# Two-layer hybrid backbone on one core: keys and values projected first, queries projected per pair of heads inside the attention loop

## The reference, cut to what matters

```python
def mla_q(cq, g, w_uq, rope):
    q = (rmsnorm(cq, g) @ w_uq).reshape(B, L, 8, 64 + 32)      # 384 -> 8 x 96
    q_nope, q_pe = q[..., :64], q[..., 64:]
    if rope is not None: q_pe = apply_rope(q_pe, ...)           # latent tokens only
    return concatenate([q_nope, q_pe], axis=-1)
def mla_kv(ckv, kpe, g, w_ukv, rope):
    kv = (rmsnorm(ckv, g) @ w_ukv).reshape(B, L, 8, 64 + 64)    # 256 -> 8 x 128
    ...                                                         # keys, values, one rotary key for all heads
def attention(q, k, v):
    s = einsum('bqhd,bkhd->bhqk', q, k) * SM_SCALE
    return einsum('bhqk,bkhd->bqhd', softmax(s), v)
```

## Time and profile before

| | us |
|---|---|
| median of 3 runs (lowest, highest) | 1796.88 (1796.58, 1798.57) |
| the profiled execution | 1798.49 |
| its span, first to last instruction | 1796.7 |
| TensorE busy | 1679.5 (93%) |
| VectorE busy | 1207.2 (67%) |
| ScalarE busy | 898.4 (50%) |

### The profile page before, as it was taken

The page is one execution under the profiler, slowest core; times in us unless marked ns, Lnnn a source line. Parts: engine busy times, 40 slices in busy tenths (PEclk is TensorE's granted clock), DMA queues, the critical chain, the costliest instruction groups (busy, mean ns, idle before and its releaser), DMA issues.

```text
span 1796.7 us, 19966 instructions
## 1 busy us (share of the span) xinstructions
PE 1679.5 (93%) x7740; PEld 1286.2 (72%) x7740; DVE 1207.2 (67%) x1598; ACT 898.4 (50%) x1032; POOL 14.2 (1%) x30
## 2 busy tenths in 40 slices
PE   5998979989999999888878999999999999999996
PEld 2774446767777777676548777878787878878775
DVE  3824554545343444483556899888898989888897
ACT  3323263322122221242355777777777777777764
POOL 1000000000000000000000000000000000000000
PEclk8999999999999999989898999999999999999998
DMA  9125211444444345232023899999998999999993
GB/s 392 58 94 212 115 67 47 169 167 153 150 141 141 117 168 185 94 133 92 24 86 141 305 361 336 345 355 351 349 345 340 358 362 348 346 342 352 361 343 115
DMA packets 55861, 402.48 MB, mean 224 GB/s; under 512 B 6416, under 2 KB 6448, under 8 KB 8784
## 3 DMA queue, kind: packets, MB, share of 16 engines
q1 hardware_dynamic: 53712, 387.47, 57.8%
q0 software_dynamic: 2048, 13.65, 2.0%
HBM read 400.05 MB, written 1.05 MB: 223 GB/s over the span
## 4 chain that ended last, share of the span: by engine, by line
PE 68%; DVE 12%; ACT 4%; issue 2%; DMA 1%; DVEq 0%; ACTq 0%
PE PS L439 19%; PE PS L441 19%; PE PS L440 19%; DVE w_lo L2268 5%; ACT w_hi L1506 3%; PE PS L449 1%; PE PS L733 1%; PE PS L1010 1%; PE PS L760 1%; DVE small L1925 1%; DVE w_lo L1629 1%; PE PS L746 1%; ACT w_hi L1131 1%; DVE arena L1938 1%; PE PS L470 1%
## 5 line engine op out<-in xcount | busy, mean ns | idle before, releaser
L2268 DVE TENSOR_TENSOR w_lo<-arena,w_hi 128x2048 fp32r<-128x2048 f32 x132 | 301.6, 2290 | 43.9 <-ACT w_hi L1506 43.9
L2268 DVE TENSOR_TENSOR w_lo<-raw,w_hi 128x2048 fp32r<-128x2048 f32 x129 | 294.9, 2290 | 32.8 <-ACT w_hi L1506 32.3
L1506 ACT CAST w_hi<-arena 128x2048 fp32r<-128x2048 f32 x132 | 251.5, 1908 | 47.0 <-PE PS L441 47.0
L1506 ACT CAST w_hi<-raw 128x2048 fp32r<-128x2048 f32 x129 | 246.8, 1916 | 44.4 <-PE PS L441 44.4
L439 PE MATMUL PS<-hT_hi,w_hi 128*128 128x512 f32 (+1 forms) x576 | 221.4, 384 | 9.3 <-DVE hT_lo L1760 8.4
L441 PE MATMUL PS<-hT_hi,w_lo 128*128 128x512 f32 (+1 forms) x576 | 215.5, 374 | 0.0
L440 PE MATMUL PS<-hT_lo,w_hi 128*128 128x512 f32 (+1 forms) x576 | 215.1, 373 | 0.0
L439 PE MATMUL PS<-w_hi,hT_hi 128*128 128x512 f32 (+1 forms) x448 | 178.3, 398 | 0.3 <-DVE w_lo L2268 0.3
L441 PE MATMUL PS<-w_hi,hT_lo 128*128 128x512 f32 (+1 forms) x448 | 174.6, 390 | 0.0
L440 PE MATMUL PS<-w_lo,hT_hi 128*128 128x512 f32 (+1 forms) x448 | 173.6, 387 | 0.0
L1629 DVE TENSOR_TENSOR w_lo<-raw,w_hi 128x2048 fp32r<-128x2048 f32 (+1 forms) x54 | 122.6, 2270 | 64.5 <-ACT w_hi L1131 64.0
(11 more groups left out here) (318 smaller groups left out, 2572.2 us busy)
## 6 DMA issues: line engine op xcount, KB each, us to landing
raw<-in_moe SPq DMA_DIRECT2D x132, 1024.0 KB, 6.7
arena<-in_moe SPq DMA_DIRECT2D x132, 1024.0 KB, 6.7
raw<-in_ada SPq DMA_DIRECT2D x45, 1024.0 KB, 4.8
raw<-in_ffn SPq DMA_DIRECT2D x33, 1024.0 KB, 4.8
raw<-in_out SPq DMA_DIRECT2D x8, 1024.0 KB, 5.5
raw<-in_inb SPq DMA_DIRECT2D x8, 960.0 KB, 5.8
raw<-in_ina SPq DMA_DIRECT2D x5, 1024.0 KB, 4.8
arena<-in_hyc POOLq DMA_DIRECT2D x2, 1920.0 KB, 11.2
```

Of the source, the lines that this page charges most:

```text
L1506: nc.scalar.copy(w_hi[:, x_slot(j), :], x_raw(n)).then_inc(x_hi, 1)
L2268: v.tensor_tensor(w_lo[:, x_slot(j), :], x_raw(NGR * (i % 2) + j), w_hi[:, x_slot(j), :].bitcast(F32), ALU.subtract).then_inc(x_lo, 1)
```

## The change

Keys are projected first, then the queries of two pairs, then the values. The other pairs are projected inside the attention loop, two pairs ahead of the pair in work, one head of the pair at a time (256 columns each, side by side in one bank). Queries are held by pair in a ring of three. VectorE saves a pair in one operation (context) or four (latent, in two parts) and does so within odd heads. The query weights and latents now have to live through the loop, so prob, probT, qtmp and qT move, probT in four pieces; the turned probabilities use banks 3 and 4, the queries 5 (pair 1: 4). POOL's last loads wait for `pv 1 3`. The rotary table holds its cosine and sine twice side by side.

```diff
-        qT = A(15616, HEADS, 512)
+        qT = A(15616, 3, 512)
-        qtmp = A(6144, 256)
-        prob = A(7936, 4, 512)
-        probT = A(9984, 4, 4, 256)
+        qtmp = A(6144, 512)
+        prob = A(11008, 4, 512)
+        probT = [A(17152, 4, 256), A(18176, 4, 256), A(14592, 4, 256), A(6656, 4, 256)]
@@ TensorE
+            def query(l, streams, pair, j):
+                s, h = attention_plan(streams)[0][2 * pair + j]
+                if j == 0:
+                    state["q"] = bank(f"q {l} {pair}", 4 if pair == 1 else 5)
+                for k in range(KQ):
+                    i = mm(state["q"][:, 256 * j:256 * j + 256], wuq[:, k, h, :], cqT[:, k, 256 * s:256 * s + 256],
+                           start=k == 0, stop=k == KQ - 1)
+                if j:
+                    i.then_inc(pe_done, 1)
+                    did(f"q {l} {pair}")
@@ TensorE, latents
-                for h in range(HEADS):
-                    o = bank(f"q {l} {h}")
-                    for k in range(KQ):
-                        i = mm(o[:, sp], wuq[:, k, h, :], cqT[:, k, sp], start=k == 0, stop=k == KQ - 1)
-                    i.then_inc(pe_done, 1)
-                    did(f"q {l} {h}")
                 for k in range(KKV):
                     eng.wait_ge(act_done, after(f"ckvTs {l} {k}"))
                 for pr in range(4):
...
+                for pair in range(2):
+                    query(l, streams, pair, 0)
+                    query(l, streams, pair, 1)
                 for t in range(NT):
@@ TensorE, attention
-                    eng.wait_ge(dve_done, after(f"qTs {l} {h}"))
+                    eng.wait_ge(dve_done, after(f"qTs {l} {n // 2}"))
...
-                    o = bank(f"pT {l} {u}", 3 + u % 3)
+                    o = bank(f"pT {l} {u}", 3 + u % 2)
...
                         ahead_to(first[n] + half + 3)
+                        if n // 2 + 2 < len(heads) // 2 and (s == 0 or half != n % 2):
+                            query(l, streams, n // 2 + 2, n % 2)
                         turn_p(n, half)
@@ VectorE
+            def save_query(l, streams, pair, part):
+                heads, units, first = attention_plan(streams)
+                q, own = qT[:, pair % 3, :], bank_of(f"q {l} {pair}")
+                if part == 0:
+                    eng.wait_ge(pe_done, after(f"q {l} {pair}"))
+                    if pair >= 3:
+                        eng.wait_ge(pe_done, after(f"s {l} {first[2 * pair - 4] - 1}"))
+                if heads[2 * pair][0] == 0:
+                    if part == 0:
+                        v.tensor_scalar(q[0:96, :], own[0:96, :], SM_SCALE, None, ALU.mult).then_inc(dve_done, 1)
+                        did(f"read q {l} {pair}", f"qTs {l} {pair}")
+                elif part == 0:
+                    v.tensor_scalar(q[0:64, :], own[0:64, :], SM_SCALE, None, ALU.mult).then_inc(dve_done, 1)
+                    did()
+                    v.tensor_tensor(q[64:96, :], own[64:96, :], ropeq[64:96, :], ALU.mult).then_inc(dve_done, 1)
+                    did()
+                else:
+                    v.tensor_tensor(qtmp[64:96, :], own[96:128, :], ropeq[96:128, :], ALU.mult).then_inc(dve_done, 1)
+                    eng.wait_ge(dve_done, did(f"read q {l} {pair}"))
+                    v.tensor_tensor(q[64:96, :], q[64:96, :], qtmp[64:96, :], ALU.add).then_inc(dve_done, 1)
+                    eng.wait_ge(dve_done, did(f"qTs {l} {pair}"))
@@ VectorE, latents: the five operations per head (L1895 to L1909) go, and in their place
+                for pair in range(2):
+                    save_query(l, streams, pair, 0)
+                    save_query(l, streams, pair, 1)
@@ VectorE, attention
                     share(u - 1)
                     n, j = units[u - 1]
+                    if n % 2 and n // 2 + 2 < len(heads) // 2:
+                        save_query(l, streams, n // 2 + 2, j)
+                        if heads[n][0] == 0:
+                            save_query(l, streams, n // 2 + 2, 1)
@@ POOL
-            eng.wait_ge(pe_done, after("s 1 15"))
-            eng.wait_ge(pe_done, after("pT 1 15"))
+            eng.wait_ge(pe_done, after("pv 1 3"))
@@ tables
-    rq[64:96, 0:256] = COS.T * SM_SCALE
-    rq[96:128, 256:512] = SIN.T * SM_SCALE
+    rq[64:96] = np.tile(COS.T * SM_SCALE, (1, 2))
+    rq[96:128] = np.tile(SIN.T * SM_SCALE, (1, 2))
```

More of the change, by code:

```diff
@@ L732, in score @@
                         q = slice(0, 512) if s else slice(256 * t, 256 * t + 256)
-                        i = mm(o[:, q], qT[0:96, h, P * t:P * t + P], KT[0:96, h, 0:512 if s else 256], start=True, stop=True)
+                        a = 256 * (n % 2) + P * (t % 2)
+                        i = mm(o[:, q], qT[0:96, (n // 2) % 3, a:a + P], KT[0:96, h, 0:512 if s else 256], start=True, stop=True)
                     i.then_inc(pe_done, 1)
@@ L760, in pv @@
                             i = mm(o[VD * j:VD * j + VD, 0:256], V[:, b, VD * (h + j):VD * (h + j) + VD],
-                                   probT[:, (2 * pair + j) % 4, b, :], start=b == 0, stop=b == nb - 1)
+                                   probT[(2 * pair + j) % 4][:, b, :], start=b == 0, stop=b == nb - 1)
                     i.then_inc(pe_done, 1)
@@ L1378, in save_turned @@
                         eng.wait_ge(pe_done, after(f"pv {l} {(n - 4) // 2}"))
-                    nc.scalar.copy(probT[:, n % 4, 2 * half:2 * half + 2, :],
+                    nc.scalar.copy(probT[n % 4][:, 2 * half:2 * half + 2, :],
                                    bank_of(f"pT {l} {u}").rearrange("p (b q) -> p b q", q=256)).then_inc(act_done, 1)
```

## The result

The changed kernel takes 1804.64 us (median of 8 runs, 1803.57 to 1812.51). The kernel before, in 8 runs on the same chip, takes 1796.99 us (1794.38 to 1798.57). The medians differ by 7.7 us. The ratio, which is taken over all runs and not from the medians, is 1.0056 with a 95% interval of 1.0043 to 1.007: three of the eight runs of the changed kernel took 1809.65 us or more, and the means differ by 10.1 us. Either way the change is slower by more than 0.2%. The profiled execution took 1804.24 us, with a span of 1802.4 us against 1796.7 before; the difference of the spans is +5.7.

A forecast was written before the change was run, and what follows sets the result against it. The prediction took the projection ahead of the loop as all TensorE time, and the loop as having holes where TensorE waits for VectorE. Layer 0's -13.1 + 19.6 and layer 1's -8.0 + 10.2 gave +8.7, 1805.5 us, range 1791 to 1815.

The forecast's parts named there:

- The front: TensorE ahead of the first score: fewer queries there, less a wait for rotary-key copies; gain 13.1 us layer 0, 8.0 layer 1.
- the clock's share: Layer 0's keys: up to 1.3 us more given back if TensorE's clock falls during the wait for ScalarE.
- The save: VectorE emptying query banks: 0.65 to 0.7 us an operation, one per context pair, four per latent pair in two parts.
- Context heads: Layer 0's loop: score 2 to score 7 +5.1 us, score 7 to turn 6 +3.3, then to head 8's transposes +4.
- A latent pair: Loop pairs with queries, two per layer: even head +1.3 us, odd head +2.5, part 1 of the save nothing; +3.8 each.
- the last two terms: Layer 0's loop: turn 6 to head 8's first transposes, taken as +4 us, and the two latent pairs, 7.2.
- Layer 1's loop: Two latent pairs with queries, the first at half clock: 6.4 and 3.8 us, together +10.2.
- The sum: Whole kernel: layer 0 +6.5 us, layer 1 +2.2, together +8.7, a median of 1805.5 us.
- the likeliest case: Whole kernel: the +8.7 us forecast, all of it slower, 1800.6 to 1811 us with the terms' ends; chance 0.48.
- The queries fill the holes: Rival, attention loops: saves delay no maxima or shares, a latent pair costs only 1.4 us; 1783.2 us, chance 0.14, partly 0.06.
- The clock stays up: Rival, attention loops: matmuls among the transposes keep TensorE's clock high, so no change; 1793.5 to 1800 us, chance 0.17.
- The new waits bring the clock down: Rival, odd heads with queries: 2.6 us waits cause three to four clock falls; 1813 to 1816 us, chance 0.15.

The follow-up runs named there:

- the run by pairs in the front: Kernel before, with layer 1's queries projected by pair ahead of the keys and saved in four 512-column operations per pair, none moved into the loop: 1789.75 us.
- the run with two turn banks: Kernel before, with only the turned probabilities put through two banks (3 and 4) instead of three: 1796.25 us, ratio 0.9995.
- the kernel without saves: Changed kernel without VectorE's query saves in the loop; all queries still projected, scores reread the first two pairs' queries: 1778.39 us, ratio 0.9907.
- the key's bank alone: Changed kernel with only the rotary key's projection put in bank 4, so no key waits for ScalarE's copies: 1804.06 us, ratio 1.0043.
- both edits: Changed kernel with latent saves one unit later and the rotary key's projection in bank 4: 1790.11 us, ratio 0.9955.

## Why the prediction was right

It said 1805.5 in a range of 1791 to 1815, slower with 0.63; the median is 1804.6. The steps:

**The front.** Predicted -13.1 and -8.0, measured -13.8 and -8.9. The keys' wait was 1.75 us, predicted 1.8, and in layer 0 the keys ran at full speed, 7.10 us, so the clock's share of up to 1.3 wasn't paid. POOL's last loads went out at 944.72, 0.4 us behind the end of the loop, and ScalarE read the router at 949.91: nothing, as predicted.

**The save.** Taken at 0.65 to 0.7 us an operation, whatever the partitions. The groups of VectorE by shape, 200 to 292 us:

```profile
L1888 DVE TENSOR_TENSOR arena<-PS,arena 32x512 f32<-32x512 f32 x4 | 2.8, 689 | 0.1
L1886 DVE TENSOR_SCALAR arena<-PS 64x512 f32<-64x512 f32 x4 | 2.7, 683 | 13.6 <-PE PS L672 13.6
...
L1883 DVE TENSOR_SCALAR arena<-PS 96x512 f32<-96x512 f32 x2 | 1.4, 688 | 6.2 <-PE PS L672 6.2
```

The columns set the time: 683 to 689 ns on 32, 64 and 96 partitions. The idle columns show VectorE waiting for the projection for 19.8 us in layer 0's loop, at six saves.

**Context heads.** Score 2 to score 7, predicted 16.4: 16.6 (206.37 to 223.00). Score 7 to turn 6, predicted 9.3: 9.4 (223.00 to 232.44), so save and split of weights do add up. Turn 6 to head 8's transposes, taken at 10.5 between 8.2 and 11.8: 9.1, nearer to the end with the clock up. The low clock came at 229.63, where it was covered. (The terms listed for the two ends add to 10.5 and 7.4 only; the turn itself is missing among them.)

**A latent pair.** Predicted +3.8, measured +4.3 (14.5 against 10.2). The even head's +1.3 is exact. The odd head's +2.5 was +3.0. About half of what is missing lies on the way from the odd head's score to its transposes, 5.36 us (262.78 to 268.14), predicted 5.1. The other half is a step taken at nothing: "Part 1 runs while the next score does: nothing". The saves of part 1, 268.12 to 269.5, hold up the split of activations and the next maximum, and the next two waits are 0.58 and 0.69 us where 0.17 and 0.80 stand without saves: 0.3 more.
The latent stretch of layer 0 as a whole, from head 8's transposes to the output projection, grew by 10.1 (50.91 against 40.80), predicted 7.2: two pairs are 8.6, and the clock of 0.68 from 241.5 to 246.8 costs 5.3 x 0.32 = 1.7 here, which in the kernel before lay ahead of head 8 and inside turn 6's stretch. So the sum of the last two terms, 11.2 predicted, was 12.8.

**Layer 1's loop.** Predicted +10.2, measured +10.4, partly by luck in the parts. The low clock at the first heads was milder (0.66 over 10 us, 3.4 us lost in the changed kernel, against 0.50 over 9.5 us, 4.75 lost), while a stretch that I had not foreseen came at the end:

```profile
889.80:899.80 10.00, 8.21 (x24) 5.65 (x25) 3.05 (x8) 3.62 (x10) 0.00 (x0) 0.66 0.00 0
940.00:946.00 6.00, 5.26 (x24) 3.57 (x25) 0.85 (x2) 2.28 (x4) 1.28 (x3) 0.52 0.11 43
```

**The sum.** The mechanism held in both loops: the wait for the projection and the save stand ahead of the maximum. That the total came within 1 us was helped by chance: the loops were 1.9 us longer than predicted, the fronts 1.5 shorter, and the same code outside them 3.4 shorter in the profiled pair. The range of the likeliest case was not added up right either: the ends that it lists give 1799.2 to 1808.8, not 1800.6 to 1811; the median lies in both.

**The rivals.** *The queries fill the holes* named the point that decides, a save plus wait of less than 1.2 us at an odd head; it was 3.6 (2.21 and 1.4). With the save moved off that point it came true in the latent pairs: an odd head's query then costs 0.1 us. *The clock stays up* did not happen in the change (0.94 and 0.87 in the loops). It happened without the saves (1.00 and 0.97). The Trainium skill (TensorE: Matmul & The Clock Gate, Part 4: PE-mode transpose) says that transposes don't count as busy as matmuls do, and by it matmuls between them would hold the clock. No run separates this: the changed kernel has those matmuls and a low clock in layer 1, 0.87 against 0.89, and the run by pairs in the front has none of them and 0.96. Nor do fewer waits explain it by themselves: the run with two turn banks has the waits of before and a clock of 0.93 in that loop. *The new waits bring the clock down* was four times possible, at the 2.72 us waits, and happened once, for a moment: behind the wait that ends at 917.35 four transposes take 1.02 us instead of 0.60 and the next score 1.91 instead of 1.02. That is 1.3 us, not three or four falls of 2.6. In layer 0 the low clock also follows the new wait of 2.50 us (at 229.63, covered) and the wait of 3.38 (from 242.66 on), where before had one fall behind 3.57; over the loop it is 0.94 against 0.93.

## What to carry to other kernels

In an engine that runs in order, a save that waits for a late producer belongs behind the work on which another engine's stall hangs, not ahead of it: an odd head's query with the same four operations to save it cost 3.0 us in one place and 0.1 in the other. Before work is moved into holes, look at which engine ends them, and place the moved work's emptying in that engine's queue by hand. And where a stall comes from an engine that empties banks, try larger operations there first: four operations for a pair in place of eight took the stall away without any move.

## What the runs showed of the hardware that was not expected

The clock's fall is not decided by a wait alone. Before and the run with two turn banks have the same waits around layer 1's first heads and 0.50 against 0.83 over 9.5 us. And the kernel without saves has nearly the same waits in layer 1 as the changed kernel: 1.34 us in the keys for ScalarE (0.54 and 1.80 there), then the same 2.03 and 0.69 us at the first transposes. Its clock stays at 1.00 from 874 to 880 us; the changed kernel's is 0.66 over the same heads. The timeline of the kernel without saves, whose rows answer to 892.00 and 892.48 of the changed kernel (0.69 and 1.92 us there):

```profile
874.62 0.41 PE L756 MATMUL PS<-ident,arena 128*128 128x128 f32 x2 [2.03 <-DVE arena L1961]
875.72 0.44 PE L756 MATMUL PS<-ident,arena 128*128 128x128 f32 x2 [0.69 <-DVE arena L1961]
876.00 1.02 PE L743 MATMUL PS<-arena 96*128 96x512 f32 x2
```

What else decides it, the runs don't tell. It makes a term of 2 to 5 us that a sum of durations can't place, and its price depends on where it falls: under a wait for VectorE it was free, 4 us later it cost 1.7, with the key's bank alone and with both edits. So a difference of a few us between two kernels, read from one trace each, is not yet the edit's.
